# Encoder block on eight cores: the convolution's shifted copies by way of a DRAM scratch, with a deeper weight ring and a reordered start

## The chip, the cores and the metric

The kernel runs on all 8 cores of one Trainium2 chip, and each core works on its own half of one of four sequences; nothing is exchanged between cores. The metric is device time in microseconds (us) of the slowest core. A core has TensorE (PE in the rows; its weight loads are PEld), VectorE (DVE), ScalarE (ACT), GpSimd (POOL) and SyncE (SP). SP, ACT and POOL can issue DMAs, and a core's 16 DMA engines carry them: SP's queue is q1 in the rows, ACT's q10, POOL's q0. TensorE's clock has two levels, 2.4 GHz (a granted clock of 1.00 in the rows) and 1.2 GHz (0.50).

## The reference

The input is `x` of shape (4, 4096, 1024) in float32. Sixteen meta tokens are put ahead of each sequence and dropped at the end.

```python
u = rms_norm(h, g_mix)
z = u @ w_in                                   # value | gate | pool | gate A | gate B
gates = sigmoid(z[..., c3:] + b_gate)
a = z[..., :c1] * sigmoid(z[..., c1:c2])       # GLU
a = depthwise_conv31(a, w_dw) + b_dw           # 31 taps over time, each channel for itself
y_conv = silu(layer_norm(a, ln_g, ln_b)) @ w_conv_out
y_pool = (multi_scale_pool(z[..., c2:c3]) @ w_pool * pool_scale) @ w_pool_out
h = h + (gates[..., :D] * y_conv + gates[..., D:] * y_pool) @ w_o
v = rms_norm(h, g_ffn)
h = h + (silu(v @ w_ffn_gate) * (v @ w_ffn_up)) @ w_ffn_down
return rms_norm(h, g_final)[:, N_META:, :]
```

## The kernel before

A core computes 2048 tokens in two passes (`i` = 0 and 1) of 1024. Channels are cut into 8 chunks of 128. Matmul operands are bf16, sums are float32.

**Start.** The first pass loads its 1055 rows of `x` as eight tiles of 128 rows and one of 31 rows (`SUBS`; the 1055 are 1024 and the halo of 31), all on SP's queue. A row tile goes through four steps, named in the list `START` by a letter and the tile's number: `A` (ScalarE squares and sums, VectorE adds epsilon, GpSimd raises to -0.5), `B` (VectorE scales it by that and by the norm weight `gb[:, 0, :]` into `ub`), `T` (TensorE transposes) and `E` (VectorE or ScalarE copies the transposed tile into `uT`). `L` loads a tile after waiting for the tile three before it, `I` issues matmuls on zeros, `G` and `H` are gate and value matmuls of chunk 0 or 1 over a third of the columns (`COLS`: 352, 352 and 351), `V` evicts such a pair into `aT`, `W` loads weights on GpSimd's queue, `C` loads the constants `pc` and two group maps, and `R` issues the shifted copies of chunk 0. A core gets 512 KB for `gb[:, 0, :]`, the same row for all 128 partitions.

**Phase 1**, by the list `P1_STEPS`: `v` is value and gate of a chunk (48 matmuls of about 352 columns), `p` the pooling columns (24 such matmuls), `c` the convolution, `w` (first pass only) the product of a pooling group's map and `w_pool_out` (8 matmuls of 512 columns), which is kept in `wpf`.

**Convolution.** `conv(c)` needs four copies of `aT`, each shifted by one more token, in the four 32-partition quarters of `rep[c % 2]`. `im2col` makes them by 16 DMAs from SBUF to SBUF, each of 32 rows of 2104 bytes, on SP's queue (chunk 0 on SP's and ScalarE's). The 31 taps then are 8 groups of 4, 64 matmuls of 512 columns. The copies of chunk c + 2 go into the buffer that conv(c) has read, so they are issued behind it.

**Group maps.** `wpool(g)` first has VectorE scale the map `wpt` by the channel scale into `wps`, two instructions, then multiplies. VectorE's queue is in program order, so the scaling stands behind all that was put on VectorE before it.

**Weights** pass through a ring of 18 tiles of 128 x 1024 bf16, each loaded from 512 KB of float32 on GpSimd's queue, which runs in program order too. `rel(k)` frees k tiles and issues up to k + 1 loads. The down projection (`down`) takes 11 tiles for each half of its columns.

Of the kernel before, what the change touches and what calls it, by code (L numbers as in the profile page):

```python
# [11 lines left out]
D = 1024  # L12
# [21 lines left out]
RING = 18  # L34
# [6 lines left out]
            "p2", "v6", "c4", "v7", "c5", "p3", "w1", "p0", "c6", "p1", "c7", "w0"]  # L41
# [3 lines left out]
START = """L3 I19 A0 B0 T0 I4 L4 A1 E0d W1 B1 T1 I4 L5 A2 E1d W1 B2 T2 A3 E2d B3 G00 T3 L6 A4 E3a W1 B4 H00 T4 L7 A5 E4d W1 B5  # L45
V00 G10 T5 L8 C0 A6 E5a W1 B6 H10 G01 T6 A7 E6d W1 B7 V10 H01 T7 A8 E7a V01 B8 G11 H11 T8 W2 E8d G02 H02 V11 V02 R0
G12 H12 V12""".split()
# [168 lines left out]
def build_nc():  # L216
# [11 lines left out]

    base0 = (nc.sbuf_base + 63) // 64 * 64
# [58 lines left out]
    wps = [m1.get(f"wps{i}", [128, 512], BF16) for i in range(2)]  # L288
# [29 lines left out]
    def sem(name):  # L318
        return nc.alloc_semaphore(name)
# [6 lines left out]
    gb_sem = [Prod(sem(f"d_gb{i}"), 16) for i in range(3)]  # L326
    wpt_sem = [Prod(sem(f"d_wpt{i}"), 16) for i in range(2)]
# [146 lines left out]
    def im2col(c, two=False):  # L474
        st = c % 2
        tot = rep_sem[st].count + 16 * 16
        for s_ in range(4):
            for j in range(4):
                o = rep[st][32 * s_:32 * s_ + 32, j, 0:REPW]
                i_ = aT[c % 3][32 * j:32 * j + 32, s_:s_ + REPW]  # L480
                S.dma((SP, ACT)[s_ % 2] if two else SP, rep_sem[st], o, i_, val=tot)
# [72 lines left out]

    def wpool(g):
        rows = [take(f"pr{2 * g + k}") for k in range(2)]
        for k in range(2):
            so, si, sc = wps[g % 2][:, k * 256:(k + 1) * 256], wpt[g % 2][:, k * 256:(k + 1) * 256], pcc(PC_PSC, 2 * g + k)
            S.op(DVE, lambda e, so=so, si=si, sc=sc: e.tensor_scalar(out=so, in0=si, scalar1=sc, scalar2=None, op0=ALU.mult),  # L559
                 [si, sc], [so])  # L560
        if g >= 2:
            wp_load(g - 2)
        for cc in range(2):
            for h in range(2):
                bw = nb()
                for k in range(2):
                    mm(psum[bw][:], wps[g % 2][:, k * 256 + cc * 128:k * 256 + cc * 128 + 128],
                       rows[k][:, h * 512:(h + 1) * 512], k == 0, k == 1, k == 1)
                wo_, wi = wpf[:, 2 * g + cc, h * 512:(h + 1) * 512], psum[bw][:]
                S.op(ACT, lambda e, wo_=wo_, wi=wi: e.activation(out=wo_, in_=wi, func=AF.Copy), [wi], [wo_])  # L570
        rel(2)
# [186 lines left out]
    zt = alloc_at("zt", [128, 512], BF16, f_start)  # L758
    s0_load(0, 0)
    S.dma(SP, cst[0], ident[:], id_d.ap())  # L760
    s0_load(0, 1)
    S.dma(SP, gb_sem[0], gb[:, 0, :], gb_d.ap()[:, 0:D])
    s0_load(0, 2)
    S.op(POOL, lambda e: e.memset(zt[:], 0.0), [], [zt[:]])
# [11 lines left out]

    rs0 = {}
# [19 lines left out]
    for st in START:  # L797
# [4 lines left out]
        elif st[0] == "C":  # L802
            S.dma(SP, cst[1], pc[:], pc_d.ap())
            wp_load(3)
            wp_load(2)
        elif st[0] == "W":
            prefetch(k)
        elif st[0] == "G":
            vb[st] = half_mm(k, int(st[2]), 1)
        elif st[0] == "H":  # L810
            vb[st] = half_mm(k, int(st[2]), 0)
        elif st[0] == "V":
            vg_evict(k, int(st[2]), (vb["H" + st[1:]], vb["G" + st[1:]]))
        elif st[0] == "I":
            idle_mm(int(st[1:]))
        elif st[0] == "R":
            im2col(k, True)
        elif st[0] == "E":
            row_e(k, DVE if st[2] == "d" else ACT)
        else:  # L820
            {"A": row_a, "B": row_b, "T": row_t}[st[0]](k)

    for i in range(NT):
# [6 lines left out]
        run_p1(i, P1_STEPS[2:])  # L830
# [180 lines left out]
```

## Time and profile before

| | |
|---|---|
| median of 3 runs | 1066.98 us (1064.65 to 1275.44) |
| the profiled execution | 1064.49 us |
| its span on the slowest core (core 1) | 1062.9 us |
| the cores' spans | 1055.2 to 1062.9 us |
| PE busy | 1018.8 us, 96% of the span |
| DVE, ACT, POOL busy | 427.8, 306.8 and 176.1 us |
| HBM read and written | 160.24 and 8.39 MB |

The profile shows the slowest core. A busy PE is a PE with a matmul in flight, so what it waits for stands in the 4% that are left, and what it loses by a lower clock is inside the busy part. "DMA share" is the mean busy share of the 16 DMA engines and can read slightly above 1. A row of waits names the engine that waited and the last releaser.

### The profile page before, as it was taken

Reading aid. Unit: us, or ns where it says so; the run is one execution under the profiler, and the core shown is the slowest. Engines: PE = TensorE matmul, PEld = TensorE weight load, DVE = VectorE, ACT = ScalarE, POOL = GpSimd, SP = SyncE. Lnnn points to the kernel's source line nnn. Section 1 sums busy time; section 2 is a strip of 40 time slices with the busy share of each in tenths; the row PEclk is TensorE's granted clock in tenths of the full one; section 3 lists DMA queues with packets and bytes.
Section 4 is the critical chain, followed back from the end, with each engine's and each line's share of the span. In section 5 each row is a group of like instructions: output and inputs, shape, how many; then the busy total and the mean of one; then the engine's idle time right before and its main releaser. Section 6 shows DMA issues by size and latency. Waiting matters only on the chain.

```text
span 1062.9 us, 17032 instructions; the slowest of 8 cores (1055.2 to 1062.9 us)
## 1 busy us (share of the span) xinstructions
PE 1018.8 (96%) x5979; PEld 502.5 (47%) x5979; DVE 427.8 (40%) x628; ACT 306.8 (29%) x530; POOL 176.1 (17%) x329
## 2 busy tenths in 40 slices
PE   5799888999999999999999999999999999999996
PEld 2455444444444444444346555544445444444442
DVE  4264444762363222321144665685336212211133
ACT  4233334622233233321112333462114311111111
POOL 3311111111113221110213111201111311111011
PEclk9899999999999999999999999999999999999999
DMA  9798785264337865551548977525433854555032
GB/s 230 126 248 160 139 172 94 44 126 60 61 109 143 152 112 93 83 78 23 77 152 190 221 155 153 93 42 119 60 57 103 139 75 75 76 74 79 1 100 99
DMA packets 59523, 116.73 MB, mean 110 GB/s; under 512 B 9714, under 2 KB 9714, under 8 KB 59440
## 3 DMA queue, kind: packets, MB, share of 16 engines
q0 software_dynamic: 38592, 70.27, 42.6%
q1 hardware_dynamic: 18160, 36.70, 11.6%
q10 hardware_dynamic: 2688, 8.67, 2.1%
q8 instruction: 50, 0.82, 0.3%
q14 instruction: 33, 0.27, 0.1%
HBM read 160.24 MB, written 8.39 MB: 159 GB/s over the span
## 4 chain that ended last, share of the span: by engine, by line
PE 92%; DMA 5%; DVE 1%; issue 1%; ACT 0%; SPq 0%; DVEq 0%; POOLq 0%; POOL 0%; ACTq 0%
PE ps L374 86%; PE ps L499 5%; DMA h<-xe 2%; DMA wr<-wst 2%; DMA xt<-xe 1%; PE ps L406 1%; DVE s L534 0%; DVE acc_s L510 0%; DVE wps L559 0%; SPq L214 0%; ACT d_sb L503 0%; DVE ub L396 0%; DVEq L892 0%; ACT psb L524 0%; ACT uT L417 0%
## 5 line engine op out<-in xcount | busy, mean ns | idle before, releaser
L374 PE MATMUL ps<-vT,wr 128*128 128x512 bf16 x1408 | 306.4, 379 | 0.0
L374 PE MATMUL ps<-uT,wr 128*128 128x352 bf16 (+2 forms) x1664 | 294.5, 336 | 4.4 <-DMA wr<-wst 3.8
L214 POOL DMA_DIRECT2D wr<-wst x268 | 142.9, 536 | 715.0 <-PE ps L374 645.4
L374 PEld LDWEIGHTS ps<-uT,wr 128*128 128x128 bf16 x1664 | 162.9, 99 | 133.6 <-issue 16.9
L374 PEld LDWEIGHTS ps<-vT,wr 128*128 128x128 bf16 x1408 | 137.1, 98 | 162.6
L374 PE MATMUL ps<-wr,fT 128*128 128x512 bf16 x704 | 153.1, 379 | 3.0 <-DMA wr<-wst 3.0
L702 DVE TENSOR_TENSOR fT<-ps,sgf 128x512 bf16<-128x512 f32 x88 | 60.9, 692 | 221.4 <-PE ps L374 196.6
L701 ACT ACTIVATE sgf<-ps 128x512 f32<-128x512 f32 x88 | 52.5, 597 | 218.6 <-PE ps L374 218.6
L374 PEld LDWEIGHTS ps<-wr,fT 128*128 128x128 bf16 x704 | 68.5, 98 | 87.3 <-issue 5.5
L722 ACT ACTIVATE sqj<-h 128x512 bf16<-128x512 f32 x32 | 20.1, 629 | 137.8 <-DVE h L720 137.8
L499 PE MATMUL ps<-rep,wr 128*32 128x512 bf16 x1024 | 58.2, 380 | 0.0
L374 PE MATMUL ps<-m2T,wpf 128*128 128x512 bf16 x256 | 57.5, 379 | 0.0
L720 DVE TENSOR_TENSOR h<-ps,h 128x512 f32<-128x512 f32 x32 | 22.1, 692 | 87.6 <-PE ps L374 87.6
L374 PE MATMUL ps<-wr,mergedT 128*128 128x512 bf16 x256 | 57.2, 379 | 0.0
L374 PE MATMUL ps<-actT,wr 128*128 128x512 bf16 x256 | 57.2, 379 | 0.0
L640 ACT ACTIVATE sgA<-ps,pc_s 128x512 f32<-128x512 f32 x32 | 21.8, 681 | 102.3 <-PE ps L374 102.3
L654 DVE SCALAR_TENSOR_TENSOR sgB<-sgB,ps 128x512 f32<-128x512 f32 x32 | 22.0, 686 | 71.3 <-PE ps L374 71.0
L467 ACT ACTIVATE sg<-ps 128x352 f32<-128x352 f32 (+1 forms) x48 | 22.1, 463 | 83.4 <-PE ps L374 56.0
L384 ACT ACTIVATE sqj<-h 128x1024 bf16<-128x1024 f32 x24 | 25.3, 1056 | 59.4 <-DVE h L683 48.8
L468 DVE SCALAR_TENSOR_TENSOR aT<-sg,ps 128x352 bf16<-128x352 f32 (+1 forms) x48 | 24.3, 520 | 39.4 <-PE ps L374 28.0
L499 PEld LDWEIGHTS ps<-rep,wr 128*32 128x32 bf16 x1024 | 25.9, 97 | 29.0 <-issue 4.6
L374 PEld LDWEIGHTS ps<-m2T,wpf 128*128 128x128 bf16 x256 | 25.1, 98 | 30.2
(67 smaller groups left out, 662.6 us busy)
## 6 DMA issues: line engine op xcount, KB each, us to landing
wr<-wst POOLq DMA_DIRECT2D x268, 256.0 KB, 4.9
rep<-aT SPq DMA_DIRECT2D x248, 65.8 KB, 4.2
xt<-xe SPq DMA_DIRECT2D x24, 512.0 KB, 4.4
out<-h ACTq DMA_DIRECT2D x15, 512.0 KB, 2.7
h<-xe SPq DMA_DIRECT2D x8, 512.0 KB, 8.7
gb_s<-gb SPq DMA_DIRECT2D x3, 512.0 KB, 5.5
wpt<-wpt SPq DMA_DIRECT2D x4, 256.0 KB, 10.5
rep<-aT ACTq DMA_DIRECT2D x8, 65.8 KB, 7.8
```

Of the source, the lines that this page charges most:

```text
L214: e.dma_start(out=o[1], in_=o[2]).then_inc(o[3], 16)
L374: S.op(PE, lambda e: e.matmul(out, lhsT=lhsT, rhs=rhs, start=start, stop=stop), [lhsT, rhs], [out], signal=signal)
L384: S.op(ACT, lambda e: e.activation(out=sqj[0:n, :], in_=src, func=AF.Square, scale=1.0 / 32.0, accum_out=ms), [src], [sqj[0:n, :], ms])
L467: S.op(ACT, lambda e: e.activation(out=sgo, in_=pgi, func=AF.Tanh, scale=0.5), [pgi], [sgo])
L468: S.op(DVE, lambda e: e.scalar_tensor_tensor(out=ao, in0=sgo, scalar=1.0, in1=pvi, op0=ALU.add, op1=ALU.mult), [pvi, sgo], [ao])
L499: S.op(PE, lambda e, o=o, lt=lt, r_=r_, q=q, j=j: e.matmul(o, lhsT=lt, rhs=r_, start=(q == 0), stop=(q == 7), tile_position=(0, 32 * j)), ...
L640: S.op(ACT, lambda e, o=o, p_=p_, bia=bia: e.activation(out=o, in_=p_, func=AF.Tanh, bias=bia, scale=0.5), [p_, bia], [o])
L654: S.op(DVE, lambda e, t=t, p_=p_: e.scalar_tensor_tensor(out=t, in0=t, scalar=1.0, in1=p_, op0=ALU.add, op1=ALU.mult), [p_, t], [t])
L701: S.op(ACT, lambda e: e.activation(out=so, in_=pgi, func=AF.Silu), [pgi], [so])
L702: S.op(DVE, lambda e: e.tensor_tensor(out=fo, in0=pui, in1=so, op=ALU.mult), [pui, so], [fo])
L720: S.op(DVE, lambda e, ho=ho, pdi=pdi: e.tensor_tensor(out=ho, in0=pdi, in1=ho, op=ALU.add), [pdi, ho], [ho])
L722: S.op(ACT, lambda e, ho=ho, sh=sh: e.activation(out=sqj[:, 0:512], in_=ho, func=AF.Square, scale=1.0 / 32.0, accum_out=sh), [ho], [sqj[:, ...
```

## The change

Five things change.

1. `im2col` stores `aT` once into a DRAM scratch (128 rows of 2110 bytes), waits on SP until it has landed, and then issues four loads, each of which fills 32 partitions by four rows of 2104 bytes each, shifted by one more token. All are on SP's queue, chunk 0's too.
2. The four scaled group maps have a buffer each. Maps 3 and 2 are scaled at the end of `START` (`S0`), which also issues the loads of maps 1 and 0 on SP; these are scaled behind `c0`. `wpool` keeps its matmuls and evictions alone, and step `w0` moves from the end of phase 1 to between `c6` and `p1`.
3. The ring has 21 tiles.
4. The norm weight comes as one row of 4 KB (`grow`), which two matmuls with ones spread over 128 partitions and VectorE copies into `gb[:, 0, :]`. The 19 matmuls on zeros ahead of tile 0 become 4 before and 4 behind these.
5. The 31-row tile (tile 8) is loaded behind tile 2, ahead of tile 3, in place of behind tile 7.

```diff
-RING = 18
+RING = 21
 P1_STEPS = [...
-            "p2", "v6", "c4", "v7", "c5", "p3", "w1", "p0", "c6", "p1", "c7", "w0"]
+            "p2", "v6", "c4", "v7", "c5", "p3", "w1", "p0", "c6", "w0", "p1", "c7"]
...
+    scr = nc.dram_tensor("scr", [2, 4, 32, EXTP], BF16, kind="Internal")
...
-    wps = [m1.get(f"wps{i}", [128, 512], BF16) for i in range(2)]
+    wps = [m1.get(f"wps{i}", [128, 512], BF16) for i in range(4)]
...
-    def im2col(c, two=False):
+    def im2col(c):
         st = c % 2
-        tot = rep_sem[st].count + 16 * 16
+        S.wait_prod(SP, rep_sem[st])
+        S.dma(SP, scr_sem[st], scr.ap()[st].rearrange("j c x -> (j c) x")[:, 0:EXT], aT[c % 3][:, 0:EXT])
+        S.wait_prod(SP, scr_sem[st])
+        tot = rep_sem[st].count + 4 * 16
         for s_ in range(4):
-            for j in range(4):
-                o = rep[st][32 * s_:32 * s_ + 32, j, 0:REPW]
-                i_ = aT[c % 3][32 * j:32 * j + 32, s_:s_ + REPW]
-                S.dma((SP, ACT)[s_ % 2] if two else SP, rep_sem[st], o, i_, val=tot)
+            o = rep[st][32 * s_:32 * s_ + 32, :, 0:REPW]
+            i_ = scr.ap()[st, :, :, s_:s_ + REPW].rearrange("j c x -> c j x")
+            S.dma(SP, rep_sem[st], o, i_, val=tot)
...
+    def wp_scale(g):
+        for k in range(2):
+            so, si, sc = wps[g][:, k * 256:(k + 1) * 256], wpt[g % 2][:, k * 256:(k + 1) * 256], pcc(PC_PSC, 2 * g + k)
+            S.op(DVE, lambda e, so=so, si=si, sc=sc: e.tensor_scalar(out=so, in0=si, scalar1=sc, scalar2=None, op0=ALU.mult),
+                 [si, sc], [so])
...
+        elif st[0] == "S":
+            wp_scale(3)
+            wp_scale(2)
+            wp_load(1)
+            wp_load(0)
```

The DMAs that SP issues up to the shifted copies of chunk 1 show changes 1, 4 and 5 (h is a tile of x, xt the 31-row tile, wpt a group map). Before:

```order
L214 DMA h_1_74<-xe 128x1024
L214 DMA gb_s<-gb 128x1024
L214 DMA h_2_75<-xe 128x1024
L214 DMA h_3_76<-xe 128x1024
L214 DMA h_4_77<-xe 128x1024
L214 DMA h_5_78<-xe 128x1024
L214 DMA h_6_79<-xe 128x1024
L214 DMA h_7_80<-xe 128x1024
L214 DMA xt_87<-xe 31x1024
L214 DMA pc_s<-pc 128x48
```

And after the change, with what each waits for:

```order
L214 DMA h_2_78<-xe 128x1024
L214 DMA xt_90<-xe 31x1024
L214 DMA h_3_79<-xe 128x1024 [waits d_xh0]
L214 DMA h_4_80<-xe 128x1024 [waits d_xh1]
L214 DMA h_5_81<-xe 128x1024 [waits d_xh2]
L214 DMA h_6_82<-xe 128x1024 [waits d_xh3]
L214 DMA h_7_83<-xe 128x1024 [waits d_xh4]
L214 DMA pc_s<-pc 128x48
```

The load of 31 rows now stands ahead of five tiles of 128 rows on the same queue. Further on in that queue, from chunk 0's copies to chunk 1's, stands after the change:

```order
L214 DMA scr<-aT_99 128x1055 [waits s_dve]
L214 DMA rep_102<-scr 32x4x1052 [waits d_scr0]
L214 DMA rep_102<-scr 32x4x1052 x3
L214 DMA wpt_105<-wpt 128x512 [waits d_wpt1,s_dve]
L214 DMA wpt_104<-wpt 128x512 [waits d_wpt0,s_dve]
L214 DMA scr<-aT_100 128x1055
L214 DMA rep_103<-scr 32x4x1052 [waits d_scr1]
L214 DMA rep_103<-scr 32x4x1052 x3
```

Where 8 + 8 DMAs on two queues made chunk 0's copies, one store, a wait for it and four loads on one queue do. On VectorE, at the convolution of chunk 1 (its sums acc_s and acc_q) and step `w3` behind it, stood before:

```order
L510 TENSOR_TENSOR acc_s<-d_sb 128x512
L512 TENSOR_TENSOR acc_q<-acc_q,sq_112 128x512
L510 TENSOR_TENSOR acc_s<-d_sb 128x512
L512 TENSOR_TENSOR acc_q<-acc_q,sq_113 128x512
L559 TENSOR_SCALAR wps_104<-wpt_102,pc_s 128x256 x2
L534 TENSOR_TENSOR s_105<-psb 128x1054
```

In the changed kernel the same place reads:

```order
L515 TENSOR_TENSOR acc_s<-d_sb 128x512
L517 TENSOR_TENSOR acc_q<-acc_q,sq_117 128x512
L515 TENSOR_TENSOR acc_s<-d_sb 128x512
L517 TENSOR_TENSOR acc_q<-acc_q,sq_118 128x512
L539 TENSOR_TENSOR s_110<-psb 128x1054
```

The scaling behind the sums is gone from here; it stands at two places further up.

## Rows read from the trace of the kernel before

**Rows 1.** The page: the clock by slice, in tenths.

```profile
PEclk9899999999999999999999999999999999999999
```

**Rows 2.** Waits of PE: engine, line, releaser; us in total, times, longest.

```profile
PE ps L374 <- DVE wps L559: 13.6, 4, 5.0
PE ps L374 <- DMA wr<-wst: 6.8, 6, 2.6
PE ps L406 <- DVE ub L396: 6.6, 3, 5.0
```

**Rows 3.** The chain that ended last: start, length in us, what.

```profile
41.44 22.12 PE ps L374 x128
63.55 3.57 PE ps L499 x64
67.12 7.27 PE ps L374 x48
...
80.79 14.33 PE ps L374 x80
...
153.15 7.12 PE ps L374 x32
...
333.00 27.63 PE ps L374 x128
```

**Rows 4.** Timeline around step w2: start, length, instruction, [idle before, releaser].

```profile
114.72 0.69 DVE L512 TENSOR_TENSOR acc_q<-acc_q,sq 128x512 f32<-128x512 f32 x1
115.33 0.61 DVE L559 TENSOR_SCALAR wps<-wpt,pc_s 128x256 bf16<-128x256 f32 x2
...
115.92 3.38 PE L374 MATMUL ps<-wr,wps 128*128 128x512 bf16 x8 [2.83 <-DVE wps L559]
```

**Rows 5.** Stretches: PE busy, granted clock, DMA share, GB/s.

```profile
40.00:47.00 7.00, 5.93 (x28) 0.53 0.87 125
...
522.00:528.00 6.00, 3.67 (x16) 1.00 1.08 152
1018.00:1020.00 2.00, 1.32 (x7) 1.00 0.14 24
```

**Rows 6.** Timeline of the start, the 31-row tile and tile 3.

```profile
14.05 1.06 ACT L384 ACTIVATE sqj<-h 128x1024 bf16<-128x1024 f32 x1 [1.21 <-DMA h<-xe]
...
20.42 0.30 SPq L214 DMA_DIRECT2D xt<-xe  x1
...
36.10 1.05 ACT L384 ACTIVATE sqj<-xt 31x1024 bf16<-31x1024 f32 x1 [6.69 <-DMA xt<-xe]
...
40.52 0.37 PE L406 MATMUL ps<-ident_s,ub 31*128 31x31 bf16 x8 [5.03 <-DVE ub L396]
```

**Rows 7.** Stretches of 1 us, columns as in rows 5.

```profile
35.00:36.00 1.00, 0.50 (x4) 1.00 0.07 15
36.00:37.00 1.00, 0.00 (x0) 1.00 0.06 18
```

**Rows 8.** DMA issues of 18 to 22 us: queue, count, KB each, us to landing.

```profile
pc_s<-pc SPq DMA_DIRECT2D x1, 24.0 KB, 16.3
```

**Rows 9.** Loads of x issued from 16 to 20 us (tile 7), by tile.

```profile
L214 SPq DMA_DIRECT2D h<-xe x1: 328/328/328, 17.2 to 17.2; - x1
...
DMA to landing us min/median/max: 8.9/8.9/8.9
```

**Rows 10.** Timeline of POOL: weight loads behind the 31-row tile's norm.

```profile
38.17 5.33 POOL L214 DMA_DIRECT2D wr<-wst  x10
```

**Rows 11.** Weight loads issued from 44 to 50 us, by tile.

```profile
DMA to landing us min/median/max: 18.9/19.7/20.3
```

**Rows 12.** First two shifted-copy DMAs of chunk 0 (47.0 to 47.6 us), by tile.

```profile
DMA to landing us min/median/max: 6.7/7.0/7.4
```

**Rows 13.** DMA queues from 62 to 66 us: packets, MB, share of 16 engines.

```profile
q0 software_dynamic: 315, 0.57, 76.0%
q1 hardware_dynamic: 318, 0.45, 35.7%
```

## What I predicted, before seeing the changed kernel's time

> **What bounds the kernel now.** I read the waits of TensorE first, since it is busy for 96% of the span. Three rows carry most of its idle time [rows 2]: 13.6 us for the scaled group maps, in four waits; 6.8 us for weights; and 6.6 us for scaled row tiles, 5.0 of it in one wait. Then the clock [rows 1]: it falls only behind such waits. In the stretch behind the 5.03 us wait the granted clock is 0.53, so nearly all of it ran at 1.2 GHz [rows 5]. The chain of waits gives the price. A matmul of 512 columns takes 27.63 / 128 = 0.216 us at the full clock and one of 352 takes 7.27 / 48 = 0.151; the 128 of 352 columns behind the long wait took 22.12 where 128 x 0.151 = 19.4 was due, so 2.7 us went to the lower clock [rows 3]. TensorE is the bound, and the change can win only in the gaps between its matmuls and in what follows them.
>
> **Step 1, the group maps.** Before w2, VectorE has the sums of the convolution's last half and then the two scalings; TensorE waits 2.83 us for these [rows 4]. The other three waits are of the same kind (the longest, at w1, stands behind a pooling chain), 13.6 us together [rows 2]. Each is followed by a slow stretch: 14.33 us for 8 matmuls of 512 and 72 of 352 columns, where 1.73 + 10.9 = 12.6 was due, so 1.7; and 7.12 for 8 and 24, where 5.35 was due, so 1.8 [rows 3]. I take 1.65 each, 6.6 for four. Scaling early removes both: **-20.2 us**. The scalings' new places hide them: four instructions, about 1.3 us by 0.61 for two [rows 4], while TensorE runs p6, and as many behind c0, where TensorE has v3's 7.3 us of work and eight PSUM banks ahead of VectorE. Without that cover it would be 1.3 us each. Moving w0 between c6 and p1 costs nothing: its weights are one step earlier in a ring that is far ahead.
>
> **Step 2, the ring.** The down projection's second half of columns needs 11 tiles; 18 - 11 = 7 are there early, and four are issued when the first half ends. From 522 to 528 us TensorE is busy for 3.67 of 6.00 us, and from 1018 to 1020 for 1.32 of 2.00 [rows 5]. With 21 tiles ten are there early, and the one that is left is needed last: 2.3 + 0.7 = **-3.0 us**, at a clock that stayed at 1.00.
>
> **Step 3, the start.** The dense work begins at 41.44 us [rows 3], behind the 31-row tile. It was issued at 20.42 and landed at 36.10 [rows 6]. What did it do in between? In its last microseconds the DMA share is 0.06 to 0.07 at 15 to 18 GB/s [rows 7], and 1/16 is 0.0625: one engine of the 16 carries all 31 rows, while a tile of 128 rows has a share on each. And what was issued behind it on SP's queue, 24 KB of constants, took 16.3 us, that is until it had landed [rows 8]. So a load behind the short tile waits for that one engine.
>
> The change puts the short tile ahead of tiles 3 to 7. Tile 7, issued at 17.2, landed 8.9 later, at 26.1 [rows 9]; the short tile then took 36.1 - 26.1 = 10.0 for its own rows, beside weight loads. Behind tile 2 (about 10 us, since 512 KB for the norm weight are gone) it holds that engine until about 20, and tile 3, which ScalarE had at 14.05 [rows 6], comes at about 22.5. The four tiles behind it keep their old distance, 26.1 - 14.05 = 12: tile 7 at about 34.5. The check by sums agrees: that one engine was done with everything at 36.1, and of its work only the norm weight's share, near 2 us, is gone. From tile 7's landing I count, from these rows where they show it and rounded otherwise: squares 1.25, the two small steps 1.1, scaling 1.3, transpose 0.6, sixteen matmuls 2.5 (0.151 each), the short tile's transpose and copy 1.0, so dense work begins at 34.5 + 7.8 = 42.3, **+0.9 us**. The bounds: if the short tile held nobody, all would come 1.5 us earlier and the 5.03 us wait shrink to 1, so 35.9 or -5.5; if its rows take turns with weights all the way, 45 or +3.5. I take +0.9 because rows 8 show the holding itself. TensorE has no wait of 5 us right ahead of the dense work any more, so that runs at 2.4 GHz: **-2.7**. Replacing 19 idle matmuls by 8 and two wide ones costs nothing: the wide ones are in float32 and slower each, so both fill about the time that tile 0 needs.
>
> The Trainium skill (DMA: Bandwidth & Descriptors, section "Why a DMA increments its semaphore by 16 and not by 1") says that a copy uses the largest number of engines up to 16 that divides the rows, one for 31 rows. The trace agrees in the 0.06 to 0.07 share. By that page alone tile 3's share would queue behind 31 rows as I have it; the sum is the same.
>
> **Step 4, the shifted copies.** Chunk 0 decides. Its values are ready about 3.3 us after the dense work's begin, and c0 is due 19.4 after it, so the copies have 16 us. Before, there were 22. The DMA engines are full then: weight loads issued from 38.17 on, ten in a row [rows 10], now thirteen, and one issued at 47 to 50 us lands 19.7 later [rows 11]. [...] And while both queues have work they take turns: 315 packets of q0 and 318 of q1 in 4 us [rows 13], so q1 gets 79 packets per us. [...] Store: 3.5 until it starts, 3.3, 1.5 to complete, 8.3 us. Loads: 0.6 for an issue, 3 to start, 13, 1.5, 18 us. Together 26.5, and c0 waits **+10.5 us**. [...] Bounds: a store like the smallest DMA (7) and loads in as little as the old copies (14.5) leave a wait of 5.5; nothing, if large DMAs get their turns in bigger portions; 14 if a round trip to DRAM adds to each stage. A wait of that length puts TensorE at 1.2 GHz again: **+2.7**. Chunk 1's copies queue behind two map loads; by then (about 75 us) the weights have caught up, and I take **+1**, up to 9. From c2 on a chunk's copies have some 14 us or more, on emptier queues: 0, at most +3 at c7 of the second pass.
>
> The skill's figure (same page, section "Anatomy of one DMA") is a fixed cost of about 2 us per DMA and the bytes at up to 436 GB/s. By it, as an estimate, store and loads take some 8 us and c0 doesn't wait; rows 12 show three times that fixed cost in this stretch, so I go by the rows.
>
> **The sum.** -20.2 - 3.0 + 0.9 - 2.7 + 10.5 + 2.7 + 1 = -10.8 us. From the profiled 1064.5 that is 1053.7. It lay 2.5 below the median, so on the median's scale 1067 - 11 = 1056.
>
> **The rivals.**
> - *The copies of chunks 0 and 1 come in time.* For it: four large DMAs instead of 16, and ScalarE no longer issues eight. Against it: rows 11 and 12. Without 10.5 + 2.7 + 1: 1042. By the page's fixed cost this is the outcome. Chance 0.22.
> - *The short tile holds nobody up*, because the hardware lets later loads pass. For it: the rows show the constants' landing, not each share's. Then -6.4 more: 1050 with the waits, 1035 without. Chance 0.12, half of it each.
> - *Slower: the round trip becomes the pace of every chunk.* Store, wait and loads of a chunk follow each other on one queue. TensorE needs 7.27 + 3.57 + 3.6 = 14.5 us per chunk [rows 3]. At a cycle of T us each of some 12 chunks waits T - 14.5, less some 24 us of head start over the two passes. From T = 19 on the kernel is over 2% slower; at 21 it is 54 us, 1110. For it: the 26.5 us above. Against it: that is for full queues, which last until about 75 us. Chance 0.07.
> - *The early waits are larger* (chunk 1 too, at 9, with a slow stretch): 1066. Chance 0.1.
> - My forecast, 1048 to 1062: 0.49.
>
> **How the numbers follow.** Range 1035 to 1068: it takes in the first two rivals and leaves out the slow one and some of the tails. About 2% (1045.6 and 1088) is what a measurement of this kernel tells from no change. Faster: 0.22, 0.06 and a low tail of 0.05, so 0.33. Slower: 0.06. Same: 0.61.
>
> **What would show it.** Waits of TensorE for wps gone and no granted clock below 1 at w3 to w0; no gap at the down projection's middle; ScalarE's squares of tile 3 near 22 us and of tile 7 near 34 to 35; a wait of the first convolution for a load of rep, near 10 us, and a slow stretch behind it. I am wrong if tile 3 comes at 13, or if c0 starts without a wait.

## The result, and the profile after

The changed kernel is **slower**: 1.0108 times the time of the kernel before, with a 95% interval of 1.0078 to 1.0137, so by some 11 to 12 us. I had forecast 1056 us, 1% faster. In two of its four executions the cores of one die ran at a lower granted clock, and such executions are left out of every ratio and median here and below. The other two took 1076.8 us (the profiled one, span 1075.2 on core 1) and 1077.41. The kernel before ran beside it at 1065.23 in the median. HBM reads rose to 176.95 MB and writes to 12.71.

| stretch of the profiled execution, us | before | after | difference |
|---|---|---|---|
| dense work of the first pass begins | 41.44 | 44.01 | +2.6 |
| dense work's 128 matmuls of about 352 columns | 22.12 | 19.25 | -2.9 |
| wait ahead of c0, and c0 itself | 0, 3.6 | 9.28, 5.70 | +11.3 |
| wait ahead of c1, and c1 itself | 0, 3.6 | 9.22, 6.54 | +12.1 |
| maps (four waits, four slow stretches) | 20.2 | 0 | -20.2 |
| second pass: waits ahead of c0 and c1 | 0 | 4.96, 3.63 | +8.6 |
| second pass: c0 and c1 themselves | 7.2 | 11.1 | +3.8 |
| down projection of both passes, and the end of the kernel | | | -3.3 |
| sum | | | +12.0 |

The profiled executions differ by 1076.8 - 1064.5 = 12.3 us, so this table explains the difference. The -3.3 is -2.8 in the first pass, -1.0 in the second and +0.5 behind the last matmul; the four waits for weights that stood in the down projection before were 3.0 us together.

The page of the kernel after: the clock by slice, and the issues of the new DMAs with KB each and the median from issue to landing.

```profile
PEclk8988999999999999999999899999999999999999
...
rep<-scr SPq DMA_DIRECT2D x64, 263.0 KB, 7.5
...
scr<-aT SPq DMA_DIRECT2D x16, 263.8 KB, 5.2
```

What TensorE waits for after (total, times, longest), to be held against [rows 2]:

```profile
PE ps L504 <- DMA rep<-scr: 22.1, 3, 9.3
PE ps L377 <- DVE uT L418: 8.3, 2, 7.8
PE ps L504 <- DVE s L539: 5.0, 1, 5.0
PE ps L409 <- DVE ub L399: 4.5, 4, 1.5
```

The row for `wps` (13.6 us) and that for `wr` (6.8 us) are gone, and a row of 22.1 us for `rep` has come. Of the 8.3 us for `uT`, 7.8 are one wait in the start, for row tile 3. The 5.0 us put down to VectorE at the same line are a fourth wait of this kind: second-pass chunk 0's loads, issued at 576.48, landed up to 16.2 us after their issue. The last was issued at 578.1, so it landed at 594.3, just before that convolution began at 594.69. On five of the eight cores all four waits are put down to the loads.

Timeline of TensorE after: start, length, instruction, idle before it and its releaser. The first rows answer to [rows 3].

```profile
44.01 19.25 PE L377 MATMUL ps<-uT,wr 128*128 128x351 bf16 x128 [0.55 <-DVE uT L418]
72.54 5.70 PE L504 MATMUL ps<-rep,wr 128*32 128x512 bf16 x64 [9.28 <-DMA rep<-scr]
...
94.72 6.54 PE L504 MATMUL ps<-rep,wr 128*32 128x512 bf16 x64 [9.22 <-DMA rep<-scr]
101.20 1.90 PE L377 MATMUL ps<-wr,wps 128*128 128x512 bf16 x8
...
594.69 5.74 PE L504 MATMUL ps<-rep,wr 128*32 128x512 bf16 x64 [4.96 <-DVE s L539]
...
611.33 5.33 PE L504 MATMUL ps<-rep,wr 128*32 128x512 bf16 x64 [3.63 <-DMA rep<-scr]
```

A convolution takes 3.64 us at the full clock. Those behind the waits take 5.3 to 6.5, so a wait costs itself and 1.7 to 2.9 us more. The map's matmuls at 101.20 follow without any gap.

SP's DMA issues after: a chunk's store, then its four loads, and two map loads between the first chunks.

```profile
47.33 0.33 SPq L214 DMA_DIRECT2D scr<-aT  x1
56.03 2.31 SPq L214 DMA_DIRECT2D rep<-scr  x4
58.50 1.14 SPq L214 DMA_DIRECT2D wpt<-wpt  x2
59.69 0.44 SPq L214 DMA_DIRECT2D scr<-aT  x1
78.86 2.52 SPq L214 DMA_DIRECT2D rep<-scr  x4
```

SP issues loads only when the store has landed, so the gaps are the stores' own round trips: 8.6 us for chunk 0, and 19.1 for chunk 1, whose store stands behind chunk 0's four loads and the two maps, 1.6 MB, on one queue. Chunk 0's loads then took 16.5 us from the first issue to c0, chunk 1's 15.9.

Weight loads from GpSimd after, in the first pass and in the second:

```profile
40.02 6.92 POOL L214 DMA_DIRECT2D wr<-wst  x13
...
563.73 7.12 POOL L214 DMA_DIRECT2D wr<-wst  x13
```

They stand 7.3 and 5.6 us ahead of the first store of their pass. (The second was there before the change as well, and I had not looked there.)

### The profile page after: what moved, and what is told of

Its sections match the earlier page's. It is cut to its first block, busy times and chain, and to the rows that moved or that the text cites. A ratio compares the mean times of both kernels' runs of the same rounds, so it can differ in the third digit from the quotient of the medians.

```text
span 1075.2 us, 16863 instructions; the slowest of 8 cores (1066.7 to 1075.2 us)
## 1 busy us (share of the span) xinstructions
PE 1022.1 (95%) x5972; PEld 505.0 (47%) x5972; DVE 429.1 (40%) x630; ACT 305.7 (28%) x530; POOL 176.1 (16%) x329
## 2 busy tenths in 40 slices
DMA packets 58612, 120.51 MB, mean 112 GB/s; under 512 B 6883, under 2 KB 6883, under 8 KB 58530
## 3 DMA queue, kind: packets, MB, share of 16 engines
HBM read 176.95 MB, written 12.71 MB: 176 GB/s over the span
## 4 chain that ended last, share of the span: by engine, by line
PE 87%; DMA 9%; SPq 1%; DVE 1%; issue 1%; ACT 0%; DVEq 0%; POOLq 0%; POOL 0%; ACTq 0%
PE ps L377 81%; PE ps L504 5%; DMA scr<-aT 5%; DMA rep<-scr 2%; DMA h<-xe 2%; PE ps L409 1%; SPq L214 1%; DVE ub L399 0%; ACT sqj L387 0%; DVEq L915 0%; DVE aT L471 0%; ACT uT L420 0%; DVE uT L418 0%; ACT sqj L727 0%; DVE h L725 0%
## 5 line engine op out<-in xcount | busy, mean ns | idle before, releaser
L504 PE MATMUL ps<-rep,wr 128*32 128x512 bf16 x1024 | 67.0, 421 | 27.1 <-DMA rep<-scr 22.1
L504 PEld LDWEIGHTS ps<-rep,wr 128*32 128x32 bf16 x1024 | 29.3, 105 | 61.8 <-issue 42.1
L727 ACT ACTIVATE sqj<-h 128x512 bf16<-128x512 f32 x32 | 20.2, 631 | 133.9 <-DVE h L725 128.7
L725 DVE TENSOR_TENSOR h<-ps,h 128x512 f32<-128x512 f32 x32 | 22.1, 692 | 82.3 <-PE ps L377 82.3
L508 ACT ACTIVATE d_sb<-ps,pc_s 128x512 f32<-128x512 f32 x32 | 22.1, 690 | 70.0 <-PE ps L504 69.9
## 6 DMA issues: line engine op xcount, KB each, us to landing
wpt<-wpt SPq DMA_DIRECT2D x4, 256.0 KB, 11.1
```

What stands on the lines that cost most here:

```text
L504: S.op(PE, lambda e, o=o, lt=lt, r_=r_, q=q, j=j: e.matmul(o, lhsT=lt, rhs=r_, start=(q == 0), stop=(q == 7), tile_position=(0, 32 * j)), ...
L508: S.op(ACT, lambda e, dso=dso, pci=pci: e.activation(out=dso, in_=pci, func=AF.Identity, bias=bia, scale=0.5), [pci, bia], [dso])
L725: S.op(DVE, lambda e, ho=ho, pdi=pdi: e.tensor_tensor(out=ho, in0=pdi, in1=ho, op=ALU.add), [pdi, ho], [ho])
```

## The experiments

The kernels were compared with the kernel before on the same chip. Two theories stood at the outset. **Backlog**: the round trips are long because the DMA engines still carry loads issued earlier. **Inherent**: a store and four loads through DRAM take this long anyway.

### The sixteen copies put back

The changed kernel with the old `im2col`:

```diff
-        S.dma(SP, scr_sem[st], scr.ap()[st]..., aT[c % 3][:, 0:EXT])
-        S.wait_prod(SP, scr_sem[st])
-            o = rep[st][32 * s_:32 * s_ + 32, :, 0:REPW]
-            i_ = scr.ap()[st, :, :, s_:s_ + REPW].rearrange("j c x -> c j x")
+            for j in range(4):
+                o = rep[st][32 * s_:32 * s_ + 32, j, 0:REPW]
+                i_ = aT[c % 3][32 * j:32 * j + 32, s_:s_ + REPW]
```

> The changed kernel with one part undone: the shifted copies are again 16 SBUF-to-SBUF DMAs per chunk (chunk 0 on SP's and ScalarE's queues); maps, ring of 21, norm weight row and early 31-row tile stay. Theory: the four waits for copies in front of c0 and c1 of both passes (9.3, 9.2, 5.0, 3.6 us) and the slow convolutions behind them (2.1, 2.9, 2.1, 1.7) are the store and loads' doing, 35.9 us in all. They vanish, and with the profile's 1076.8 the kernel takes 1041 (1036 to 1048). Rival: the waits come from the DMA engines being full of weights (a ring of 21 and a later start), so that any kind of copy is late; then at least 15 us of the 36 stay and it takes 1056 or more.

Measured: 1044.95 us, ratio 0.9804 (0.9782 to 0.9827). Its TensorE timeline:

```profile
44.02 22.02 PE L374 MATMUL ps<-uT,wr 128*128 128x351 bf16 x128 [0.55 <-DVE uT L415]
65.97 3.64 PE L499 MATMUL ps<-rep,wr 128*32 128x512 bf16 x64
...
76.81 3.64 PE L499 MATMUL ps<-rep,wr 128*32 128x512 bf16 x64
```

The same burst of weight loads, the same start and the same map order, and c0 and c1 wait for nothing on this core; on the other seven TensorE waits 0.6 to 2.5 us for `rep` in all. Against this kernel the scratch costs 1077 - 1045 = 32 us; the table's four waits with their slow convolutions are 35.8, less 2.8 because the dense work ran at the full clock in the changed kernel and not here (19.25 and 22.02 us), which makes 33. So one of the five edits takes more than the other four give.

### The scratch alone

The kernel before with only its `im2col` replaced by the new one.

> The kernel before with one part of the change alone: the shifted copies by store, wait and four loads. Theory: the price of the copies by way of DRAM is 25 to 36 us also without the other four changes, since weight loads fill the DMA queues at the same places (ten in a row at 38 us, thirteen at 563 us): 1090 to 1101. In front of c0 and c1 of both passes stand waits for rep. Rival: the copies are late only because of the ring of 21 and the later start, then it costs under 10 us: below 1075.

Measured: 1088.86 us, ratio 1.0210 (1.0188 to 1.0231), slightly under the expected span. Waits of TensorE, and its first convolutions:

```profile
PE ps L504 <- DMA rep<-scr: 18.2, 3, 7.8
```

```profile
70.42 6.02 PE L504 MATMUL ps<-rep,wr 128*32 128x512 bf16 x64 [7.76 <-DMA rep<-scr]
...
83.64 3.64 PE L504 MATMUL ps<-rep,wr 128*32 128x512 bf16 x64
```

Besides these two TensorE waits 5.2 us at c0 and at c1 of the second pass. The scratch alone gives +2.1% and the other edits alone -2.0%, yet together they give +1.1%: the effects don't add. Here c1 of the first pass doesn't wait, against what was expected. Its store lands sooner (issued at 56.57, its loads at 72.42: 15.9 us where the changed kernel has 19.2), and its loads take up to 6.1 us to land where the changed kernel has 15.9 to c1. Three things differ at this place: no map loads stand in front of the store, the ring of 18 sends ten weight loads in a row and not thirteen, and TensorE is slower. Which of them counts wasn't tested.

### The maps alone

The kernel before with the early scaling and the new place of w0, with nothing else.

> The kernel before with one part of the change alone: four buffers for the scaled group maps, scaled early, and w0 between c6 and p1. Theory: this is worth the four waits and the slow stretches behind them, 20.2 us: ratio 0.981, 1045 to 1048. Rival: without these pauses the copies (16 DMAs a chunk) or the weights become late and give back over 5 us: 1050 or more.

Measured: 1051.11 us, ratio 0.9849 (0.9827 to 0.9871), 16 us gained where the expected 1045 to 1048 asked for 18 to 21. One row of the waits of the slowest core (core 0, span 1050.5 us) says part of the reason:

```profile
PE ps L374 <- DMA wr<-wst: 8.0, 5, 3.8
```

The slowest core before waited 6.8 us for weights, so this is 1.2 more; but the longest of these waits, 3.8 us in the down projection, has a slow stretch of 2.6 us behind it (36.40 where 33.83 was due), and 1.9 us of waits for `rep` have come. The other seven cores have spans of 1039.2 to 1044.8 us, so the median of this kernel is set by one core. With 21 tiles, in the kernel with the copies put back, the wait for weights isn't there, and the four other edits together give 21 us.

### The store on another queue

The changed kernel with the store issued by ScalarE:

```diff
-        S.wait_prod(SP, rep_sem[st])
-        S.dma(SP, scr_sem[st], ...)
+        S.wait_prod(ACT, rep_sem[st])
+        S.dma(ACT, scr_sem[st], ...)
```

> The changed kernel with the store into the scratch issued by ScalarE instead of SP, the four loads still by SP. Theory: chunk 1's store landed 19.1 us after its issue because it stood behind chunk 0's loads and two maps in SP's queue. On a queue of its own it lands within 10, the waits at c1 (9.2 and 3.6 us) shrink to under 2 each and the one at c0 of the first pass stays at 7 or more: 1058 to 1066. Rival: the queue does not matter, a store to DRAM takes as long wherever it is issued, since the engines share out their time by bytes: within 3 us of the changed kernel.

Measured: 1081.95 us, ratio 1.0147 (1.0124 to 1.0170), no better than the changed kernel. A miss in the total, with the mechanism right for the store alone. The first two stores (issues, KB, median to landing, from 47 to 80 us) and the waits:

```profile
scr<-aT ACTq DMA_DIRECT2D x2, 263.8 KB, 9.0
```

```profile
PE ps L504 <- DMA rep<-scr: 29.7, 6, 10.4
```

Chunk 1's store takes 8.7 us instead of 19.1, so the other 10 were its own queue. But little of that reaches TensorE. Chunk 1's loads, issued at 62.38 in place of 78.86, now take up to 27.6 us to land, and c1 begins at 92.16 for 94.72, 2.6 us sooner. Its wait halves, 4.35 for 9.22, in part because c0 waits longer, 10.45 for 9.28. Six waits appear, also at c2 and c7, and the sum grows from 27.1 to 29.7. ScalarE's program order isn't the reason at c7 of the first pass: chunk 7's store was issued at 155.93 us in both kernels. It took 6.6 us to land here, and there its loads were issued 4.0 us behind it; why it was slower stays open.

### Weight loads made to wait

A first try, in which a release of ring tiles recorded fewer loads at a time:

> The changed kernel with the ring's refill spread out: releases issue as many weight loads as they free until c2 of a pass, then one more each as before, and the 11 tiles freed at the end of the down projection are not reloaded in one burst but a step at a time from c2 of the second pass on. The computation is the same. Theory: the copies by way of DRAM are late because SP's queue takes turns with a backlog of weight loads; with a smaller backlog chunk 0's copies take under 20 us from the store's issue in place of 25, the waits at c0 and c1 fall from 18.5 to under 8 us in the first pass and from 8.6 to under 2 in the second, and the kernel takes 1048 to 1062. Rival: the round trip through DRAM is slow by itself (a store of some 5 us and loads of 10 or more even on quiet queues), then it stays within 5 us of the changed kernel.

Measured: 1078.75 us, ratio 1.0113 (1.0088 to 1.0139). It tests nothing: the slots were long free, so nothing held a load back, and GpSimd still issued 13 in a row at 40.45 us. The waits (9.78, 6.25, 5.42 and 5.63) sum to 27.1 us, as in the changed kernel.

So GpSimd was then made to wait for TensorE's progress before each refill in phase 1. Until c2 it refills no tile ahead, and the tiles that the end of the down projection frees aren't refilled at once:

```diff
+        if pace["gate"]:
+            S.wait_prod(POOL, PE)
-        prefetch(k + 1)
+        prefetch(k + pace["extra"])
```

> The changed kernel, the same computation; in phase 1 of both passes GpSimd now waits for TensorE before each ring slot is refilled (so the 13 weight loads at 40.0 and at 563.7 us are issued one at a time), refills none ahead until chunk 2's convolution, and the slots that the down projection frees are not refilled in one go. Theory (the store and the four loads stand behind the loads of weights that share the DMA engines): the round trip of chunk 0 drops from 25 us to 12 to 17, chunk 0's wait from 9.3 to 0 to 2, chunk 1's from 9.2 to 0 to 3, the second pass's from 5.0 and 3.6 to 0 to 1, with their slow stretches mostly gone: 1041 to 1050 us in all (1077 less some 27 to 35). Rival (a store and four loads of 2 KB rows take this long by themselves, at 3 to 5 us of transfer each and a fixed cost each): waits over 7 us remain at chunk 0 and the time is within 5 of 1077. Risk: waits for wr appear where loads come too late; each is named by the profile.

Measured: 1085.7 us, ratio 1.0186 (1.0164 to 1.0207), **slower still**. This was my theory's main test, and its total fell. In the trace it splits in three. The DMAs issued from 45 to 53 us, with the packets of both queues:

```profile
q0 software_dynamic: 156, 0.28, 25.9%
q1 hardware_dynamic: 254, 0.49, 16.7%
...
wr<-wst POOLq DMA_DIRECT2D x5, 256.0 KB, 10.0
rep<-scr SPq DMA_DIRECT2D x4, 263.0 KB, 10.4
scr<-aT SPq DMA_DIRECT2D x1, 263.8 KB, 2.6
```

and in the changed kernel, from 45 to 57 us:

```profile
q0 software_dynamic: 893, 1.62, 97.3%
q1 hardware_dynamic: 144, 0.27, 7.0%
...
scr<-aT SPq DMA_DIRECT2D x1, 263.8 KB, 8.6
```

First, the store of chunk 0: 2.6 us on engines that are nearly idle, and 8.6 in the stretch in which the weights' queue carries 1.6 MB. The backlog is shown as its cause, and a store to DRAM is not slow in itself. The Trainium skill (DMA: Bandwidth & Descriptors, section "Anatomy of one DMA") gives about 2 us fixed and the bytes at up to 436 GB/s for a DMA issued by GpSimd. Worked out from that, as an estimate, 0.27 MB take 2.6 us. On idle engines this case's trace agrees, for a store issued by SP; under load the same store took 8.6 to 20.1.

Second, TensorE's timeline in this kernel:

```profile
67.16 6.52 PE L508 MATMUL ps<-rep,wr 128*32 128x512 bf16 x64 [4.25 <-DMA rep<-scr]
...
84.28 6.49 PE L508 MATMUL ps<-rep,wr 128*32 128x512 bf16 x64 [3.33 <-DMA rep<-scr]
...
179.68 4.90 PE L508 MATMUL ps<-rep,wr 128*32 128x512 bf16 x64 [7.56 <-DMA rep<-scr]
...
693.41 5.72 PE L508 MATMUL ps<-rep,wr 128*32 128x512 bf16 x64 [6.56 <-DMA rep<-scr]
```

The waits of c0 and c1 fall from 18.5 to 7.6 us, and in the second pass from 8.6 to 0.5. But chunk 0's loads still take up to 14.8 us (the tiles that the first matmuls free are refilled right beside them), and chunk 1's store 20.1.

Third, the loads that were held back come later, and the waits with them, at c6 and c7 (in the second pass at c4, c5 and c7): from 140 to 185 us as many weight loads are issued as in the changed kernel, 15, and they land in 16.1 us instead of 8.5, behind refills that catch up; chunk 7's store, issued at 146.31, takes 16.8. In all TensorE waits 33.4 us for `rep` in eight places. **The waits moved and didn't shrink.** How full the engines are shows in the share of the first pass's phase 1, from 44 to 180 us, for the kernel before, the changed one and the one with the copies back, in this order:

```profile
44.00:180.00 136.00, 122.43 (x1067) 69.01 (x1065) 65.55 (x85) 50.54 (x93) 21.12 (x40) 0.94 0.83 167
```

```profile
44.00:180.00 136.00, 117.49 (x1056) 67.23 (x1056) 63.45 (x81) 47.12 (x90) 23.53 (x45) 0.92 0.96 186
```

```profile
44.00:180.00 136.00, 135.98 (x1156) 77.65 (x1157) 73.54 (x104) 55.64 (x104) 28.12 (x51) 0.97 0.91 181
```

The last three numbers are granted clock, DMA share and GB/s. The gated kernel has a share of 0.95 over the same stretch, though its engines stood idle from 45 to 49 us. So what was held back there had to be caught up in a stretch with little room. That this is why the waits moved is argued and not shown: a gate that is less strict at the start might leave less to catch up.

### Bytes or a second trip

The copies of before, with the store added ahead of them. The copies don't wait for it and nothing reads it (SP waits only for the store of two chunks earlier), so it has the changed kernel's bytes and not its second trip in series.

```diff
+        S.wait_prod(SP, scr_sem[st])
+        S.dma(SP, scr_sem[st], scr.ap()[st]..., aT[c % 3][:, 0:EXT])
         tot = rep_sem[st].count + 16 * 16
```

> The kernel with the sixteen copies of before and all other edits of the change, to which each chunk's store to the DRAM scratch is added ahead of its copies; nothing reads the scratch and the copies don't wait for it, so the computation is the same and 0.26 MB per chunk, as many bytes as the changed kernel's, go through the same DMA engines. Theory A (the second trip in series costs the time: the loads can't be issued before the store has landed): 1045 to 1050 us, 0 to 5 over the kernel without the store, and no wait for rep over 3 us. Theory B (the bytes cost it, since the DMA engines are busy for nearly all of phase 1): 1060 to 1075 us, with waits for rep of 10 us or more in all.

Measured: 1053.96 us, ratio 0.9898 (0.9879 to 0.9916), between the two theories: 9 us over the kernel without the store (10 by the ratios). The trace places most of them:

```profile
65.49 3.64 PE L504 MATMUL ps<-rep,wr 128*32 128x512 bf16 x64
...
80.67 6.16 PE L504 MATMUL ps<-rep,wr 128*32 128x512 bf16 x64 [4.28 <-DMA rep<-aT]
```

One wait, at c1, of 4.28 us with 2.5 of slow convolution and 1.1 of slow matmuls behind it, and none for `rep` at c0 or in the second pass. So of the scratch's 32 us about 9 come from the added bytes and their place in the queue. The other 23 are what is left. The two kernels differ there in the wait for the store, but also in what the copies read (SBUF or DRAM), in their number and in the queues of chunk 0, and no run takes these apart.

The changed kernel's rows speak for the wait. Had chunk 0's loads been issued at 47.33, when the store was, and taken the same 16.5 us, they would have landed at 63.8, and c0 was due at 72.54 - 9.28 = 63.3, so it would have waited some 0.5 us. For chunk 1 the same estimate gives 59.69 + 15.9 = 75.6, and c1 was due at 85.5. The loads by themselves are little slower than the sixteen copies, which took 14.8 us in the kernel before, from 47.0 us to the last landing.

### The 31-row tile

Three kernels, all with the sixteen copies. One has the tile loaded by two DMAs:

```diff
-        S.dma(SP, sm, buf[0:n, :], xe.ap()[row0:row0 + n, :])
+        if n == 31:
+            S.dma_parts(SP, sm, [buf[0:16, :], buf[16:31, :]], [xe.ap()[row0:row0 + 16, :], xe.ap()[row0 + 16:row0 + 31, :]])
+        else:
+            S.dma(SP, sm, buf[0:n, :], xe.ap()[row0:row0 + n, :])
```

> The kernel of e1_copies_back with the 31-row tile loaded by two DMAs of 16 and 15 rows in place of one of 31, at the same early place. Theory: the 31 rows sit on one DMA engine and hold up tiles 3 to 7 behind them; split they are spread over 16 and 15 engines, tile 3 reaches ScalarE near 13 us in place of 22.95, dense work begins near 37 in place of 44, and the kernel takes 6 to 8 us less than e1_copies_back. Rival: the start is set by the work per tile on ScalarE and VectorE (about 3 us a tile), so tile 3 comes earlier but dense work begins no more than 2 us earlier.

Measured: 1041.55 us in the median, ratio 0.9786 (0.9744 to 0.9828). ScalarE's first row of tile 3 and TensorE's dense work in it:

```profile
13.67 1.06 ACT L391 ACTIVATE sqj<-h 128x1024 bf16<-128x1024 f32 x1 [1.70 <-DMA h<-xe]
```

```profile
37.64 19.25 PE L381 MATMUL ps<-uT,wr 128*128 128x351 bf16 x128 [0.55 <-DVE uT L422]
```

and tile 3 in the changed kernel:

```profile
22.95 1.06 ACT L387 ACTIVATE sqj<-h 128x1024 bf16<-128x1024 f32 x1 [11.37 <-DMA h<-xe]
```

In the changed kernel's wait for tile 3 the engines as a whole do next to nothing (columns as in [rows 5]):

```profile
21.00:23.00 2.00, 0.00 (x0) 0.50 0.07 18
```

With two DMAs tile 3 comes 9.3 us sooner, and the dense work 6.4 us sooner than with one (37.64 for 44.02). That a transfer of 31 rows on one engine holds up the tiles behind it is shown. The Trainium skill (DMA: Bandwidth & Descriptors, section "Why a DMA increments its semaphore by 16 and not by 1") has a DMA run on the largest number of engines up to 16 that divides its rows. By that rule 16 and 15 rows use 16 and 15 engines where 31 use one; the time of tile 3 agrees.

End to end it is 3.4 us of the 6 to 8 expected, and the intervals of the two kernels overlap, so the gain isn't clear of noise. Part of the 6.4 us is given back: in the profiled execution (1049.2 us, the longest of those counted) TensorE waits 3.3 us for `rep` and 2.3 for weights, which the kernel with one DMA doesn't on its slowest core.

The second has the tile back behind tile 7, in one DMA:

> The kernel of e1_copies_back with the 31-row tile loaded behind tile 7 again. Theory: ahead of tiles 3 to 7 the short tile costs more than it brings. Behind them tile 3 reaches ScalarE near 13 us, the short tile lands near 34 to 36, dense work begins at 38 to 41 in place of 44.0, maybe with a slow stretch of 2.7 us behind the wait; 1 to 6 us less than e1_copies_back. Rival: its late landing is the dearer of the two and it takes 2 us more or worse.

Measured: 1043 us, ratio 0.9778 (0.9759 to 0.9797). On core 4 the dense work begins at 39.81 us, behind a wait of 3.8. The same core began it at 43.94 with the tile in the early place. So that place, meant for the start, costs it 4.1 us. End to end 1.9 us are left, and here too the intervals overlap.

The third combines the split with the first, idle form of pacing:

> The kernel of e2_short_split with the ring's refill spread out as in e5_paced. Theory: the copies' 16 small DMAs then have a queue of their own nearly, the waits of 3.3 us for rep of e2_short_split vanish, and it takes 1037 to 1041. Rival: these waits come from the pace at which SP issues 16 DMAs (0.58 us each), then nothing changes.

Measured: 1040.62 us, ratio 0.9749 (0.9720 to 0.9779). TensorE still waits 2.5 us for `rep`, so that wait didn't vanish. The split with real gating:

> The kernel with the sixteen copies of before and all other edits of the change, with the 31-row tile loaded as 16 and 15 rows, and with the same gating of weight loads: same computation. Theory: nothing waits for rep or wr in phase 1; 1035 to 1041 us, 0 to 4 less than the split one without gating. Rival (the copies were in time anyhow): same as the split kernel within 2 us. Where weights then come late (wr named by the waits, over 5 us), it is 3 to 8 slower than it.

Measured: 1042.16 us, ratio 0.9779 (0.9763 to 0.9795). The intervals of the three kernels with a split tile and of the one with the late tile overlap, so the four can't be told apart. Gating gains nothing, and the expectation that nothing waits was wrong: TensorE waits 4.1 us for `rep` and 5.2 for weights in the profiled execution.

### The change as meant, with both mends

The scratch, the split tile and the gate together:

> The changed kernel with both mends, the 31-row tile as 16 and 15 rows and the gated weight loads, with the scratch copies kept: same computation. Theory: dense work starts at 37.6 to 39; the round trip of chunk 0 now has less time before it is wanted only by what the clock gives, and costs 0 to 3 us, chunk 1 0 to 3: 1037 to 1045 us, and within 5 of the kernel with sixteen copies that runs beside it. Rival (the round trip itself is too long): over 1060.

Measured: 1076.88 us, ratio 1.0109 (1.0090 to 1.0127), 35 us over the kernel with the copies beside it. My theory is refuted in its strong form. Dense work starts at 38.67, 5.3 us sooner than in the changed kernel, and all of it is given back at waits ahead of convolutions, 31.7 us in six places where the changed kernel has 27.1 in four. The largest is at c7:

```profile
171.83 5.15 PE L518 MATMUL ps<-rep,wr 128*32 128x512 bf16 x64 [9.74 <-DMA rep<-scr]
```

## Why the prediction was wrong, step by step

The forecast for the profiled execution was 1053.7 us, and it took 1076.8: 23.1 too low.

**Right.** Step 1, the maps: -20.2 forecast. From c1's start to the end of phase 1 the time fell from 102.86 to 85.55 us although c1 itself took 2.9 longer, so -20.2. Step 2, the ring: -3.0 forecast; the 3.0 us of waits are gone, -3.3 with what follows them. The dense work at the full clock: -2.7 and -2.9, though this is luck in part. The forecast made the wait of 5 us ahead of it the reason for the slow stretch; but before the change core 4 took 19.25 us for that work behind a wait of 2.96, and in the kernel with the copies put back, where no such wait is left, core 3 took 22.02. Tile 3 at 22.5 forecast, 22.95 measured, because a load behind the short tile waits for the one engine.

**Step 3, the start, undersized.** +0.9 forecast, +2.6 measured. The landing of tile 3 was right, but I let tiles 4 to 7 keep their distance from it. Tile 7 landed at 31.1 us and not at 34.5. Its squares still began at 34.80, since ScalarE was behind with the tiles before it, so that number came out by luck. From there to the dense work I counted 7.8 us and it took 9.2. The largest part that I left out is a wait of 1.12 us: the short tile's scaling, which the sum had at nothing, began only at 41.70, behind an eviction into `aT` on VectorE, when TensorE had done its sixteen matmuls at 42.0.

```profile
43.12 0.35 PE L409 MATMUL ps<-ident_s,ub 31*128 31x31 bf16 x8 [1.12 <-DVE ub L399]
```

**Step 4, chunk 0, right.** +10.5 and +2.7 forecast, +9.3 and +2.1 measured. The store took 8.6 us (8.3 forecast), and the loads 16.5 (18 forecast). The terms inside these sums are another matter. The 3.3 us for the store's packets and the 13 for the loads' come from two packets for a row of 2104 bytes, 256 and 1024, and no run shows that. Nor does one show the 3.5, 3 and 1.5 us for starting and completing a DMA by themselves. The stretch of the store shows 144 packets for its 128 rows, so it is one per row and 16 small ones per DMA; and the two pages of the profile agree, with 9714 packets under 512 bytes before and 6883 after, 2831 fewer for 176 fewer DMAs, which is 16 each. The loads are 576 packets and not 1024. (The 14.5 us that the bounds give the old copies fit the 14.8 measured.) The other input was wrong too, and the two nearly cancel: I let SP's queue pass 79 per us [rows 13]; from 60 to 66 us after, it passed 53:

```profile
q0 software_dynamic: 361, 0.66, 71.3%
q1 hardware_dynamic: 315, 0.60, 32.8%
```

Taking turns holds again, 361 to 315, but here, where the packets of SP's queue are larger (1.9 KB in the mean for 1.4), a turn took longer. So the new `im2col` saves next to no packets (store and loads 720 per chunk, sixteen copies of 48 packets 768), and its packets are larger.

**Step 4, chunk 1: the step that failed first.** The forecast said "by then (about 75 us) the weights have caught up" and took +1, up to 9. Measured +9.2 and 2.9. So the term of +1 measured +12.1. Its reason, that the weights have caught up, failed: from 79 to 85 us their queue still took 89.0% of the engines' time, and the engines ran out of work only at about 95 us. And two things were missing. I counted the store's landing for chunk 0 alone, when every chunk has it in series. And chunk 1's store stands behind 1.6 MB of its own queue, which is 10 of its 19.1 us; but the store on ScalarE's queue brought c1 only 2.6 us forward, so the place in the queue is the smaller part.

**The second pass: the step that failed second.** The forecast had 0 from c2 on, "at most +3 at c7 of the second pass", and left c0 and c1 of the second pass unexamined, and they cost 8.6 us of waits and 3.8 of slow convolutions, 12.4. The burst of 13 weight loads at 563 us stood in the trace before, where I had looked only at 38.17. With real gating these waits fall to 0.5 us, so there the backlog is needed for them. But it isn't enough: with the sixteen copies and the same burst neither convolution waits.

**The rivals.** "The early waits are larger" (chunk 1 too, 1066, chance 0.1) was the nearest; with the second pass in it, it would have said about 1078. "The round trip becomes the pace of every chunk" was wrong for the changed kernel, whose c2 to c7 don't wait in either pass, but c7 waits in both kernels with a gate. "The copies of chunks 0 and 1 come in time" was wrong: both waited 9.2 to 9.3 us, and only the sixteen copies come in time. "The short tile holds nobody up" was wrong by tile 3 at 22.95.

**What stays open.** The split of the scratch's 32 us into 9 and 23 rests on one kernel, and the dead store also delays the copies behind it, so its 9 are bytes and order together; the 23 are a remainder, most of it the second trip by the estimate above. A gate that holds the weights back only around the first two stores, and gives them back in small steps, wasn't tried.

## What to carry to other kernels

Where the DMA engines are as busy as here (a share of 0.83 before the change), cost a DMA by what has been issued ahead of it, on its own queue and on the others, and count each landing that the next issue waits for. Sending the copies through DRAM cost this kernel 32 us, 9 of them for a quarter more bytes per chunk and the rest mostly for the second trip in series. Fewer and larger DMAs were no gain here, where TensorE hadn't waited for the sixteen issues. Look for bursts in every pass of a loop, since a pattern read off the first pass can stand in the second one ahead of a different reader; and where a resource is nearly full, expect that spreading loads in time can move a wait instead of removing it, as it did here.

The best version found keeps the sixteen copies, scales the maps early, has the ring of 21 and loads the short tile as 16 and 15 rows: 1041 to 1042 us, 0.975 to 0.979 of the kernel before. Leaving that tile behind tile 7 can't be told from it (1043 us, 0.978).

## What the runs showed of the hardware that I had not expected

- The landing of one and the same DMA, a store of 0.26 MB to DRAM, took 2.6 us on idle engines, 8.6 behind weight loads, 8.7 and 9.4 on ScalarE's queue, which carried only such stores then, and 19.1 and 20.1 behind 1.6 MB of its own queue.
- Each store showed 16 packets more than its rows (144 for 128), so a row of 2110 bytes is one packet, and 176 DMAs fewer came with 2831 packets under 512 bytes fewer. Two queues with work got about the same number of packets, 53 and 60 per us with the large DMAs and about 79 with the small copies.
- The dense work of 128 matmuls took 19.25 us on four cores of one execution of the kernel with the copies put back, 20.1 to 20.2 on three and 22.02 on one, each time behind the same waits of 1.12 and 0.55 us. So a single reading of such a stretch is uncertain by nearly 3 us.
